# Hybrid trunk on one core: the second delta mixer's tail merged with the second triangular inverse, and sixteen steps of memory pieces in the second layer's first mixer

## The chip, the core and the metric

The kernel runs on one core of a Trainium2 chip. Its engines work side by side and meet at semaphores: TensorE (PE, matrix products), VectorE (DVE), ScalarE (ACT), GpSimd (POOL, unused here) and SyncE (SP), whose queue issues the weight transfers in order. The time is that of the device for one execution, in microseconds (us); before the change three runs gave a median of 1926.84 us (1923.26 to 1929.85).

## The reference, cut to what matters

Two decoder layers over 256 tokens of width 1024. Each layer projects its input once, runs four mixers on groups of 256 columns, projects their outputs, attends to a memory of 256 tokens and ends with a feed-forward part (dense, then experts).

```python
for l in range(DEPTH):
    p = rmsnorm(x, norm_mix[l]) @ w_in[l]
    y_a = hgrn2_mixer(...)          # first mixer: gated linear recurrence, levels of doubling width
    y_b = gated_deltanet_mixer(...) # second: needs (I + lower)^-1 per chunk and head
    y_c = rglru_mixer(...)          # RG-LRU: elementwise scan
    y_d = rwkv7_mixer(...)          # RWKV-7: needs a second inverse of the same kind
    x = x + concatenate([y_a, y_b, y_c, y_d]) @ w_out[l]
    k, v = mem_n @ xattn_wk[l], mem_n @ xattn_wv[l]     # depends on the memory alone
    x = x + cross_attention(rmsnorm(x, norm_xattn[l]), k, v)
    x = x + (swiglu(...) if l % 2 == 0 else moe_swiglu(...))
# delta rule inside y_b, per chunk: u, w = solve((I + lower), [v*b, k*b*exp(g)])
# v_new = u - w @ state ; o = (q*exp(g)) @ state + scores @ v_new ; state = decay*state + k^T @ v_new
```

## The kernel before

Every engine has its own program, written out by hand in one order; there is no scheduler. `ahead(n)` on ACT and DVE splits weight chunks up to number n: a chunk arrives as f32 in one of three buffers `raw`, ACT rounds it into `whi`, DVE puts the rest into `wlo` by a subtraction (128x2048), and PE multiplies with both. SP's queue loads chunks and memory pieces in the order of `plan_chunks`; a load waits until the buffer's user of three loads earlier is done: for a chunk that is `w_lo` (DVE's subtraction), for a memory piece `kv_done` (its last matmul).

**Memory pieces.** Keys and values of the memory are computed in eight pieces per layer, numbered 0 to 7 here, each of eight steps `kv(l, i, ks)`. A step is two matmuls of 128x256; it depends on nothing but the piece's load, and so it is put on PE wherever PE would wait. `kv_put(l, i)` is ACT's copy of a finished piece. Piece 6 is worked off in the RWKV tail. The load order around it is, in layer 0: piece 3, output chunk 0, piece 4, piece 5, output chunk 1, piece 6, chunks 2 and 3; in layer 1: piece 4, output chunk 0, piece 5, output chunk 1, piece 6, chunks 2 and 3. So in layer 0 output chunk 1 takes the buffer of output chunk 0 and piece 6 follows it on the queue; in layer 1 piece 6 itself takes the buffer of output chunk 0.

**The mixers.** `hgrn(l)` is the first mixer with seven levels. Then `inverse(2l)` inverts the delta mixer's 64x64 triangles and `inverse(2l+1)` RWKV's. An inverse has an entry (transposes, a first group) and levels 1 to 6. In a level PE forms the inner products (`inv_t`), DVE masks them (`inv_t1`), PE forms the outer ones (`inv_p`), DVE adds them to X (`inv_xy`) and ACT copies Y (`inv_c`), for two groups g. `after(v)` on PE and DVE's `beside(v)` are other work of the level. Between the inverses stood the delta mixer's tail, a serial chain on PE, DVE and ACT: `solve(6, 0)` -> ACT copies (`gd_us`) -> state -> DVE masks (`state_bd`) -> `gd_km` -> DVE subtracts (`gd_r1`) -> `solve(6, 1)` -> ACT -> `outputs` -> squares -> `head_ss`. RWKV's operands were formed on DVE (`rwkv_operands`), and its first scores (`rk_sc`) and their mask (`inv_n`) started the second inverse. After that inverse comes the RWKV tail, again a chain, with the steps of piece 6 between its parts.

In layer 0, `hgrn` held sixteen steps (pieces 0 and 1, four ahead of the levels), in layer 1 eight. The low part of output chunk 0 was made on DVE in level 1 of the second inverse:

```python
                    if v == 1:
                        ahead(first_chunk["w_out", l] + 1)
```

Of the kernel before, what the change touches and what calls it, by code (L numbers as in the profile page):

```python
# [14 lines left out]
P = 128  # L15
# [3 lines left out]
TT = SEQ // P  # L19
# [90 lines left out]
def build(nc, A, out):  # L110
# [14 lines left out]
    with ExitStack() as ctx:  # L125
# [188 lines left out]


# [92 lines left out]
        KV_BANK = [[7, 6, 7, 7, 7, 7, 2, 1], [3, 1, 7, 7, 7, 7, 2, 3]]  # L408
# [67 lines left out]
        def _(act):  # L476
# [180 lines left out]
            def hgrn(l):
                for v in range(LEVELS):
# [29 lines left out]
                    if v == 6:  # L688
                        kv_put(l, 1 + l)
# [22 lines left out]
            def head_rms(l):  # L712

                act.wait_ge(S("o_full"), 2 * l + 2)
                a(tmp(6), ps[:, 6, :], ACT.Square).then_inc(S("o_sq"), 1)
                act.wait_ge(S("rk_ops"), l + 1)
                act.wait_ge(S("o_ss"), 2 * l + 2)
                a(tmp(7), ps[:, 5, :], ACT.Ln, scale=1.0 / HD, bias=epsc(0))
                a(tmp(7), tmp(7), ACT.Exp, scale=-0.5).then_inc(S("o_rn"), 1)
                inverse_turned(2 * l + 1)  # L720
                inverse_first(2 * l + 1)
                table("natural_log")

# [15 lines left out]
            def deltanet(l):  # L739
                inverse_level(2 * l, 2)  # L740
                kv_put(l, 2 + l)
# [7 lines left out]
                kv_put(l, 3 + l)  # L749
                for t in range(TT):  # L750
                    act.wait_ge(S("gd_u"), 2 * l + t + 1)
                    a(tmp(6)[:, 256 * t:256 * t + 256], ps[:, 6, 256 * t:256 * t + 256], ACT.Copy).then_inc(S("gd_us"), 1)
                head_rms(l)
                inverse_level(2 * l + 1, 1)
                kv_put(l, 4 + l)
                inverse_level(2 * l + 1, 2)
                inverse_level(2 * l + 1, 3)
                inverse_level(2 * l + 1, 4)
                inverse_level(2 * l + 1, 5)
                ahead(first_chunk["w_out", l] + 2)  # L760
# [207 lines left out]
        def _(dve):  # L968
# [305 lines left out]
            def inverse(i, after=None):  # L1274

                N, X, Y, T1 = mt(3), X_INV, mt(5), mt(0)
                for v in range(LEVELS):
                    for g in range(2):
                        s_ = slice(256 * g, 256 * g + 256)
                        if v == 0:  # L1280
                            for u in HALVES:
                                tt(many(T1[u, s_]), many(N[u, 512 * g:512 * g + 512])[:, :, u], rep(level_b(0)[u], 4), ALU.mult)
                            tt(many(Y[:, s_]), rep(ident_b[:, :], 4), many(T1[:, s_]), ALU.subtract).then_inc(S("inv_xy"), 1)
# [38 lines left out]

            def rwkv_operands(l):

                tt(pt(B_K), K_KK, K_EM, ALU.mult).then_inc(S("rk_kb"), 1)
                tt(pt(A_I), pt(D_R), K_E, ALU.mult)
                tt(cm(pt(B_V))[:, :, 0:P], cm(pt(D_K))[:, :, 0:P], cm(pt(A_Q))[:, :, 0:P], ALU.mult)
                tt(cm(pt(B_V))[:, :, P:], cm(pt(D_R))[:, :, P:], cm(pt(A_Q))[:, :, P:], ALU.mult)
                tt(cm(pt(C_X))[:, :, 0:P], cm(K_KA)[:, :, 0:P], cm(pt(A_Q))[:, :, 0:P], ALU.mult)
# [1171 lines left out]
```

## Time and profile before

| | us |
|---|---|
| three runs, median | 1926.84 (1923.26 to 1929.85) |
| the profiled execution | 1923.63 |
| its span, first to last instruction | 1921.8 |
| PE busy | 1844.5 |
| DVE busy | 1436.4 |
| ACT busy | 1153.5 |
| mean granted TensorE clock | 0.988 of full |

The mixers of layer 0 lie at 113.8 to 262 us of the span, those of layer 1 at 652.8 to 795; projections, attention and feed-forward fill the rest, the experts from 915 on. A row of a timeline gives start, duration, engine, line, what is written from what, and in brackets the engine's idle time before it with what ended it. One f32 matmul shows as two records.

### The profile page before, as it was taken

To read this page: it belongs to the slowest core of one execution; us is meant where nothing else is said; L and a number is where in the kernel's file an instruction comes from. 1 tells how busy PE (TensorE), PEld (TensorE's weight loads), DVE (VectorE), ACT (ScalarE), POOL (GpSimd) and SP (SyncE) were. 2 spreads that over 40 slices of the span, in tenths; PEclk is the share of its full clock that TensorE was granted. 3 is DMA by queue.
4 is the path that set the end of the run, shared out by engine and by line. 5 is a ranking of instruction groups with operands and counts; after the bars stand their busy time and mean duration, and the time that the engine had idled before them with its cause. 6 is when DMAs were issued, how large, how long until landed. Compare 5 with 4: busy or idle time off the path is not lost.

```text
span 1921.8 us, 30255 instructions
## 1 busy us (share of the span) xinstructions
PE 1844.5 (96%) x12776; PEld 1589.5 (83%) x12777; DVE 1436.4 (75%) x1475; ACT 1153.5 (60%) x1129; POOL 0.2 (0%) x4
## 2 busy tenths in 40 slices
PE   7999999999999988996999999999999999999996
PEld 6988789999999877895788888888888888888884
DVE  6876654544458876545889989899898998989985
ACT  6565344434344653444677777677776777767774
POOL 0000000000000000000000000000000000000000
PEclk9999999999999999998999999999999999999998
DMA  7512224455555211234799999999999999999992
GB/s 247 162 60 68 68 88 168 164 189 181 176 173 172 66 46 68 88 132 167 288 365 368 361 333 377 350 370 365 326 386 341 365 372 332 382 364 340 371 374 87
DMA packets 239452, 466.02 MB, mean 242 GB/s; under 512 B 11856, under 2 KB 87760, under 8 KB 239312
## 3 DMA queue, kind: packets, MB, share of 16 engines
q1 hardware_dynamic: 239168, 463.93, 67.6%
q8 instruction: 103, 1.69, 0.4%
q14 instruction: 37, 0.30, 0.0%
q10 hardware_dynamic: 144, 0.11, 0.0%
HBM read 462.95 MB, written 1.05 MB: 241 GB/s over the span
## 4 chain that ended last, share of the span: by engine, by line
PE 92%; DVE 6%; issue 1%; ACT 1%; DVEq 0%; DMA 0%; ACTq 0%
PE ps L2265 32%; PE ps L1696 16%; PE ps L2275 16%; PE ps L1681 15%; PE ps L1716 8%; PE ps L2321 2%; PE ps L2296 1%; PE ps L1761 1%; DVE MT L974 1%; PE ps L2336 1%; DVE TMP L974 0%; DVE MT L977 0%; DVE hT_lo L980 0%; DVE MT L1216 0%; PE ps L1786 0%
## 5 line engine op out<-in xcount | busy, mean ns | idle before, releaser
L1458 DVE TENSOR_TENSOR wlo<-raw,whi 128x2048 fp32r<-128x2048 f32 x140 | 320.5, 2291 | 55.8 <-ACT whi L843 55.6
L843 ACT ACTIVATE whi<-raw 128x2048 fp32r<-128x2048 f32 x140 | 268.9, 1922 | 120.8 <-PE ps L2275 71.3
L987 DVE TENSOR_TENSOR wlo<-raw,whi 128x2048 fp32r<-128x2048 f32 x85 | 194.5, 2289 | 83.8 <-ACT whi L494 83.7
L1458 DVE TENSOR_TENSOR wlo<-PT,whi 128x2048 fp32r<-128x2048 f32 x84 | 192.1, 2292 | 31.2 <-ACT whi L843 30.2
L494 ACT ACTIVATE whi<-raw 128x2048 fp32r<-128x2048 f32 x85 | 162.2, 1908 | 80.1 <-PE ps L1716 31.9
L2265 PE MATMUL ps<-whi,hE_hi 128*128 128x512 f32 x672 | 185.4, 398 | 2.4 <-DVE hE_lo L1527 2.4
L843 ACT ACTIVATE whi<-PT 128x2048 fp32r<-128x2048 f32 x84 | 161.4, 1922 | 34.8 <-PE ps L2265 34.2
L2265 PE MATMUL ps<-wlo,hE_hi 128*128 128x512 f32 x672 | 180.1, 390 | 0.0
L2265 PE MATMUL ps<-whi,hE_lo 128*128 128x512 f32 x672 | 179.8, 389 | 0.0
L2265 PEld LDWEIGHTS ps<-wlo,hE_hi 128*128 128x128 f32 x672 | 126.2, 188 | 27.2
L2265 PEld LDWEIGHTS ps<-whi,hE_lo 128*128 128x128 f32 x672 | 126.1, 188 | 26.7
L2265 PEld LDWEIGHTS ps<-whi,hE_hi 128*128 128x128 f32 x672 | 122.0, 188 | 24.8 <-DVE hE_lo L1527 2.6
L2275 PE MATMUL ps<-whi,act_hi 128*128 128x512 f32 x336 | 130.8, 389 | 1.4 <-DVE act_lo L1502 1.4
L2275 PE MATMUL ps<-whi,act_lo 128*128 128x512 f32 x336 | 130.8, 389 | 0.0
L2275 PE MATMUL ps<-wlo,act_hi 128*128 128x512 f32 x336 | 130.7, 389 | 0.0
L1696 PE MATMUL ps<-hT_hi,whi 128*128 128x256 f32 x848 | 120.8, 285 | 0.0
L1696 PE MATMUL ps<-hT_hi,wlo 128*128 128x256 f32 x848 | 119.0, 283 | 0.0
L1696 PE MATMUL ps<-hT_lo,whi 128*128 128x256 f32 x848 | 119.0, 283 | 0.0
L1696 PEld LDWEIGHTS ps<-hT_hi,whi 128*128 128x128 f32 x848 | 110.1, 192 | 2.3 <-issue 1.4
L1696 PEld LDWEIGHTS ps<-hT_lo,whi 128*128 128x128 f32 x848 | 109.4, 192 | 0.0
L1696 PEld LDWEIGHTS ps<-hT_hi,wlo 128*128 128x128 f32 x848 | 109.4, 192 | 0.0
L485 ACT ACTIVATE MT<-ps 128x256 f32<-128x256 f32 (+2 forms) x94 | 43.9, 467 | 104.8 <-PE ps L1696 51.6
(301 smaller groups left out, 3337.8 us busy)
## 6 DMA issues: line engine op xcount, KB each, us to landing
raw<-in_moe_w_up SPq DMA_DIRECT2D x111, 1024.0 KB, 7.1
PT<-in_moe_w_down SPq DMA_DIRECT2D x56, 1024.0 KB, 6.7
PT<-in_moe_w_gate SPq DMA_DIRECT2D x55, 1024.0 KB, 7.0
TMP<-in_moe_w_gate SPq DMA_DIRECT2D x55, 1024.0 KB, 6.9
raw<-in_moe_w_down SPq DMA_DIRECT2D x55, 1024.0 KB, 5.9
raw<-in_w_in SPq DMA_DIRECT2D x28, 1024.0 KB, 5.5
raw<-in_ffn_w_gate SPq DMA_DIRECT2D x11, 1024.0 KB, 5.4
raw<-in_ffn_w_up SPq DMA_DIRECT2D x11, 1024.0 KB, 5.5
```

The costliest lines, as they stand in the source:

```text
L485: return chain.link(lambda: nc.scalar.activation(o, i, f, **kw))
L494: nc.scalar.activation(whi[i % SPL][:, :], raw[d % RAW][:, :], ACT.Copy).then_inc(S("w_hi"), 1)
L843: nc.scalar.activation(ex_hi[m % XSPL], ex_raw[m % XRAW], ACT.Copy).then_inc(S("w_hi"), 1)
L974: return chain.link(lambda: V.tensor_tensor(o, x0, x1, op))
L987: V.tensor_tensor(wlo[i % SPL][:, :], raw[d % RAW][:, :], whi[i % SPL][:, :].bitcast(F32), ALU.subtract).then_inc(S("w_lo"), 1)
L1458: V.tensor_tensor(ex_lo[m % XSPL], ex_raw[m % XRAW], ex_hi[m % XSPL].bitcast(F32), ALU.subtract).then_inc(S("w_lo"), 1)
L1681: return Signalled(pe.matmul(o, lhsT, rhs, start=start, stop=stop, skip_group_check=True))
L1696: ins = pe.matmul(ps[:, bank, SEQ * m:SEQ * m + SEQ], wp[a_][:, k, P * m:P * m + P], src[b_][:, k, :], start=i == 0 and k == 0, stop=last)
L1716: ins = pe.matmul(ps[:, 4 + 2 * t + hf, :], src(b_, kk, t), wp[a_][:, kk, 512 * hf:512 * hf + 512], start=first and kk == 0 and i == 0, st ...
L2265: ins = pe.matmul(ps[:, bank, :], h_[b_][:, X_K * i + k, :], wp[a_][:, k, :], start=i == 0 and n_ == 0 and k == 0, stop=i == 1 and n_ == 2 ...
L2275: ins = pe.matmul(ps[:, 4 + hf, :], act_[b_][:, P * (TM_ROWS * i + kk):P * (TM_ROWS * i + kk) + P], wp[a_][:, kk, 512 * hf:512 * hf + 512] ...
L2321: ins = pe.matmul(g_tokens(c), xs[:, t, P * c:P * c + P], oneh[:, P * t:P * t + P], start=t == 0, stop=t == 1)
```

## The change

1. The delta mixer's tail moves into the levels of the second inverse: PE does `solve(6, 0)` at v 0, the state at v 1, `gd_km` at v 2, `solve(6, 1)` at v 3, `outputs` at v 4, `head_ss` at v 5. DVE's and ACT's parts move with it. Y of the second inverse gets another place (`y_work`), because `mt(5)` still holds the first inverse's result; the delta output is copied out of PSUM (`g_out`).
2. RWKV's first scores are made at the end of the first inverse, in bank 4, and its operands are spread over DVE's `beside`.
3. In layer 1 the pieces are dealt as in layer 0: pieces 2 and 3 in `hgrn` (sixteen steps), piece 4 from there to level 2 of the first inverse, none at its levels 3 to 6, piece 5 in the second inverse. In layer 0 pieces 4 and 5 both lie in the second inverse.
4. The splits of the output chunks move: DVE's low part of chunk 0 stands after the second inverse, chunk 1's after the RG-LRU work, which in turn stands after the RWKV state's mask; ACT's split of chunk 1 stands in the RWKV tail.

The load order of SP is the same. The diff, cut to its core:

```diff
@@ ACT
-                    if v == 3:
-                        rel_part(l, 0)
-                        if l == 0:
-                            kv_put(0, 0)
+                    if v == 3:
+                        rel_part(l, 0)
+                        kv_put(l, 2 * l)
...
             def rwkv(l):
+                i = 2 * l + 1
+                inverse_turned(i)
+                inverse_first(i)
+                gdn_right(l, 0)
+                inverse_level(i, 1)
...
+                inverse_level(i, 3)
+                gdn_right(l, 1)
+                inverse_level(i, 4)
+                act.wait_ge(S("o_full"), 2 * l + 2)
+                a(tmp(6), ps[:, 6, :], ACT.Square)
+                a(g_out(l), ps[:, 6, :], ACT.Copy).then_inc(S("o_sq"), 1)
+                inverse_level(i, 5)
...
+                        act.wait_ge(S("y_put"), 4 * l + 2)
+                        ahead(first_chunk["w_out", l] + 2)
                     act.wait_ge(S("rk_u"), 2 * l + t + 1)
@@ DVE, rwkv
                     if v == 0:
-                        head_out(l, 1, ps[:, 6, :], tmp(7), lambda c: pc("gdn_norm", l), pt(B_Z), 1)
+                        tt(pt(A_I), pt(D_R), K_E, ALU.mult).then_inc(S("rk_kb"), 1)
...
                     if v == 1:
-                        ahead(first_chunk["w_out", l] + 1)
+                        dve.wait_ge(S("state"), 3 * l + 2)
...
                     if v == 2:
                         mask(l, 1, 4, mt(1), strict).then_inc(S("rk_m"), 1)
+                        dve.wait_ge(S("gd_km"), l + 1)
+                        tt(tmp(4)[:, 256:512], tmp(4)[:, 256:512], ps[:, 6, 256:512], ALU.subtract).then_inc(S("gd_r1"), 1)
...
+                mask(l, 0, 4, mt(3), strict).then_inc(S("inv_n"), 1)
                 inverse(2 * l + 1, after=beside)
+                ahead(first_chunk["w_out", l] + 1)
+                head_out(l, 1, g_out(l), tmp(7), lambda c: pc("gdn_norm", l), pt(B_Z), 1)
+                dve.wait_ge(S("state"), 3 * l + 3)
...
                 rglru(l, LEVELS)
                 chain.settle()
                 ahead(first_chunk["w_out", l] + 2)
@@ PE, hgrn and deltanet
-                    if l and 1 <= v < 5:
-                        kv(1, 2, [v + 3])
-                    if l == 0 and v < 2:
-                        kv(0, 0, range(5, 8) if v else [4])
-                    if l == 0 and 2 <= v < 6:
-                        kv(0, 1, [2 * v - 4, 2 * v - 3])
+                    if v < 2:
+                        kv(l, 2 * l, range(5, 8) if v else [4])
+                    if 2 <= v < 6:
+                        kv(l, 2 * l + 1, [2 * v - 4, 2 * v - 3])
...
+                    if v == LEVELS - 1:
+                        pe.wait_ge(S("rk_kb"), 2 * l + 1)
+                        scores(4, pt(B_Q), pt(B_K)).then_inc(S("rk_sc"), 1)
@@ PE, rwkv
+                k4 = ([0, 1, 2], [3, 4], [5, 6, 7], [], [], [], [])
+                k5 = ([], [], [], [0, 1, 2], [3, 4], [5], [6, 7]) if l == 0 else ([0], [1], [2], [3], [4], [5], [6, 7])
```

**The order on DVE, layer 0, second inverse.** Before, level 1 and the beginning of level 2; `wlo` is the low part of output chunk 0.

```order
L974 TENSOR_TENSOR MT<-ps,con16b 128x256 [waits y_put,inv_t]
L974 TENSOR_TENSOR MT<-ps,con16b 128x256 [waits inv_t1,inv_t]
L987 TENSOR_TENSOR wlo<-raw,whi 128x2048 [waits w_hi]
L974 TENSOR_TENSOR MT<-MT,ps 128x256 [waits inv_t1,inv_p]
L974 TENSOR_TENSOR MT<-MT,ps 128x256 [waits inv_xy,inv_p]
L974 TENSOR_TENSOR MT<-ps,con16b 128x256 [waits inv_xy,inv_t]
L974 TENSOR_TENSOR MT<-ps,con16b 128x256 [waits inv_t1,inv_t]
L980 SCALAR_TENSOR_TENSOR MT<-ps,con 128x1024 [waits inv_t1,rk_sc]
```
Now, the end of that inverse (level 6, RWKV's last mask, the two copies that end the inverse) and what follows.

```order
L986 TENSOR_SCALAR MT<-ps 64x256 [waits inv_xy,inv_t]
L986 TENSOR_SCALAR MT<-ps 64x256 [waits inv_t1,inv_t]
L989 SCALAR_TENSOR_TENSOR MT<-ps,con 128x1024 [waits inv_t1,rk_sc]
L1311 COPY MT<-ps 64x256 [waits rk_m,inv_p]
L1311 COPY MT<-ps 64x256 [waits inv_xy,inv_p]
L996 TENSOR_TENSOR wlo<-raw,whi 128x2048 [waits w_hi]
L983 TENSOR_TENSOR TMP<-spare_hi_50,TMP 128x512 [waits inv_xy,o_rn]
L989 SCALAR_TENSOR_TENSOR TMP<-TMP,par,PT 128x256 [waits dve_step] x2
L1210 CAST hT_hi<-TMP 128x512 [waits dve_step]
```
The subtraction of 128x2048 moved from between the products and the adds of level 1 to behind the last copy.

**The order on PE, layer 0, from level 6's second group to piece 6.** `memT,raw` or `raw,memT` of 128x256 are steps; the transposes are `con,PT`. Before:

```order
L1681 MATMUL ps<-MT 64x64 [waits inv_t1,inv_c]
L1681 MATMUL ps<-MT 64x64 x3
L1684 MATMUL ps<-con,PT 128x128 [waits y_put]
L1684 MATMUL ps<-con,PT 128x128 x3
L1681 MATMUL ps<-raw,memT 128x256 [waits raw_in1,rk_m,inv_xy]
L1681 MATMUL ps<-raw,memT 128x256 x3
L1681 MATMUL ps<-TMP,MT 128x64 [waits rk_vk]
L1681 MATMUL ps<-TMP,MT 128x64 x3
```
Now:

```order
L1689 MATMUL ps<-MT 64x64 [waits inv_t1,inv_c]
L1689 MATMUL ps<-MT 64x64 x3
L1689 MATMUL ps<-raw,memT 128x256 [waits raw_in2,raw_in1]
L1689 MATMUL ps<-raw,memT 128x256 x3
L1692 MATMUL ps<-con,PT 128x128 [waits o_rn]
L1692 MATMUL ps<-con,PT 128x128 x3
L1689 MATMUL ps<-raw,memT 128x256 [waits rk_ops,raw_in1,rk_m,inv_xy]
L1689 MATMUL ps<-raw,memT 128x256 x3
L1689 MATMUL ps<-TMP,MT 128x64 [waits rk_vk]
```
Two steps of piece 5 stand between the level and the transposes, and the first steps of piece 6 wait on `rk_ops` too; they wait for their load (`raw_in1`) in both.

**The order on PE, layer 0, the entry of the second inverse.** `PT` of 128x128 are RWKV's first scores, `MT,con` of 64x64 the transposes behind the mask. Before:

```order
L1681 MATMUL ps<-PT 128x128 [waits rk_kb]
L1681 MATMUL ps<-PT 128x128 x7
L1681 MATMUL ps<-TMP,con 128x512 [waits o_sq]
L1681 MATMUL ps<-raw,memT 128x256 [waits raw_in1]
L1681 MATMUL ps<-raw,memT 128x256 x3
L1681 MATMUL ps<-MT,con 64x64 [waits inv_n]
L1681 MATMUL ps<-MT,con 64x64 x15
```
Now, from piece 3's last steps on, at the end of the first inverse:

```order
L1689 MATMUL ps<-memT,raw 128x256 [waits raw_in2,kv_put]
L1689 MATMUL ps<-memT,raw 128x256 x3
L1689 MATMUL ps<-PT 128x128 [waits rk_kb]
L1689 MATMUL ps<-PT 128x128 x7
L1689 MATMUL ps<-MT,con 64x64 [waits inv_n,inv_xy]
L1689 MATMUL ps<-MT,con 64x64 x15
```
Between scores and transposes stood the sums of squares (`TMP,con`) and two steps of piece 4; now they follow each other.

## Rows read from the trace of the kernel before

**Rows 1.** Page, part 1: engine, busy us, share, instructions.
```profile
PE 1844.5 (96%) x12776; PEld 1589.5 (83%) x12777; DVE 1436.4 (75%) x1475; ACT 1153.5 (60%) x1129; POOL 0.2 (0%) x4
```

**Rows 2.** Stretches: length, busy us (instructions) by engine, PE clock, DMA share, GB/s.
```profile
113.80:149.80 36.00, 32.29 (x425) 26.98 (x425) 29.39 (x55) 17.80 (x32) 0.00 (x0) 0.95 0.20 61
...
184.30:235.30 51.00, 46.92 (x812) 38.56 (x810) 28.22 (x52) 15.81 (x28) 0.00 (x0) 1.00 0.25 84
652.80:689.30 36.50, 27.64 (x393) 22.95 (x392) 29.96 (x56) 17.19 (x31) 0.00 (x0) 0.86 0.11 31
...
725.70:767.90 42.20, 37.34 (x772) 31.68 (x771) 27.81 (x51) 15.50 (x27) 0.00 (x0) 1.00 0.21 77
```

**Rows 3.** Timeline of SP's queue (start, us): chunk 1 and piece 6, both layers.
```profile
208.91 0.37 SPq L431 DMA_DIRECT2D raw<-in_w_out  x1
209.32 0.47 SPq L431 DMA_DIRECT2D raw<-in_xattn_wv  x1
...
748.37 0.37 SPq L431 DMA_DIRECT2D raw<-in_xattn_wv  x1
```

**Rows 4.** Transfers at piece 6, layer 0, then layer 1: KB, us from issue to landing.
```profile
raw<-in_xattn_wv SPq DMA_DIRECT2D x1, 1024.0 KB, 7.4
...
raw<-in_xattn_wv SPq DMA_DIRECT2D x1, 1024.0 KB, 5.2
```

**Rows 5.** Timeline of PE, layer 0, delta tail, second inverse, piece 6.
```profile
186.22 1.28 PE L1681 MATMUL ps<-TMP,MT 64*64 64x64 f32 x16
...
195.55 1.16 PE L1681 MATMUL ps<-PT 64*128 64x128 f32 x16
...
197.60 1.89 PE L1681 MATMUL ps<-raw,memT 128*128 128x256 f32 x8
199.42 1.15 PE L1681 MATMUL ps<-MT,con 64*64 64x64 f32 x32
...
205.00 1.48 PE L1681 MATMUL ps<-MT 64*64 64x64 f32 x34
...
209.51 1.13 PE L1681 MATMUL ps<-raw,memT 128*128 128x256 f32 x4 [1.16 <-ACT vA L485]
...
222.68 1.22 PE L1681 MATMUL ps<-MT 64*64 64x64 f32 x64 [0.15 <-DVE MT L974]
...
231.22 2.46 PE L1681 MATMUL ps<-MT 64*64 64x64 f32 x32
233.62 0.66 PE L1684 MATMUL ps<-con,PT 128*128 128x128 f32 x4
235.32 3.63 PE L1681 MATMUL ps<-raw,memT 128*128 128x256 f32 x8 [1.04 <-DVE MT L1301]
```

**Rows 6.** Timeline of PE, layer 1, second inverse: a bare level, and piece 6.
```profile
752.43 2.52 PE L1681 MATMUL ps<-MT 64*64 64x64 f32 x96 [1.07 <-DVE MT L974]
...
767.86 1.14 PE L1681 MATMUL ps<-raw,memT 128*128 128x256 f32 x2 [1.04 <-DVE MT L1301]
```

**Rows 7.** Timeline of ACT, layer 1, first inverse: the copies of level 4.
```profile
716.62 0.86 ACT L485 ACTIVATE MT<-ps 128x256 f32<-128x256 f32 x2
```

**Rows 8.** Timeline of DVE, layer 0, second inverse and what follows.
```profile
206.60 2.28 DVE L987 TENSOR_TENSOR wlo<-raw,whi 128x2048 fp32r<-128x2048 f32 x1
...
231.93 0.96 DVE L977 TENSOR_SCALAR MT<-ps 64x256 f32<-64x256 f32 x2 [3.19 <-PE ps L1681]
233.00 1.23 DVE L980 SCALAR_TENSOR_TENSOR MT<-ps,con 128x1024 f32<-128x1024 f32 x1
234.32 0.94 DVE L1301 COPY MT<-ps 64x256 f32<-64x256 f32 x2
235.37 0.69 DVE L974 TENSOR_TENSOR spare_lo<-spare_lo 128x512 f32<-128x512 f32 x1
```

**Rows 9.** Stretches as in rows 2: at piece 6 of layer 0, and at the router.
```profile
235.50:238.90 3.40, 3.40 (x10) 2.66 (x10) 3.23 (x6) 0.09 (x1) 0.00 (x0) 0.50 0.01 2
901.10:914.80 13.70, 5.47 (x26) 5.32 (x27) 11.99 (x35) 1.49 (x2) 0.00 (x0) 0.50 0.43 140
```

More of the change, by code:

```diff
@@ L313, in build, with y_work, g_out @@
         X_INV, NT, NC = H(1), H(8), H(9)
+        def y_work(i):
+            return g_rel(i // 2)[:, 0:512] if i % 2 else mt(5)[:, 0:512]
+        def g_out(l):
+            return g_rel(l)[:, 512:1024]
         def col(a, n=1):
@@ L1386, in beside @@
+                    if v == 3:
+                        tt(cm(pt(B_V))[:, :, 0:P], cm(pt(D_K))[:, :, 0:P], cm(pt(A_Q))[:, :, 0:P], ALU.mult)
+                        tt(cm(pt(B_V))[:, :, P:], cm(pt(D_R))[:, :, P:], cm(pt(A_Q))[:, :, P:], ALU.mult)
                     if v == 4:
                         mask(l, 2, 4, PT[:, 0:1024], incl).then_inc(S("rk_m"), 1)
+                    if v == 5:
+                        tt(K_B, pt(D_R), pt(D_K), ALU.mult)
+                        for c in range(2):
+                            s_ = slice(256 * c, 256 * c + 256)
+                            ts(K_B[:, s_], K_B[:, s_], pc("rwkv_r_k", l, c), ALU.mult).then_inc(S("rk_ops"), 1 if c else 0)
@@ L1979, in head_ss @@
                 pe.wait_ge(S("o_sq"), 2 * l + which + 1)
-                mm(ps[:, 5 if which else 6, :], bdones, squares).then_inc(S("o_ss"), 1)
+                mm(ps[:, 6, :], bdones, squares).then_inc(S("o_ss"), 1)
             def inverse(i, after=None):
-                N, X, Y, T1 = mt(3), X_INV, mt(5), mt(0)
+                N, X, Y, T1 = mt(3), X_INV, y_work(i), mt(0)
                 SWAPPED = tuple(zip(HALVES, HALVES[::-1]))
@@ L2077, in deltanet @@
-                solve(6, 0, tmp(4)).then_inc(S("gd_u"), 1)
-                pe.wait_ge(S("kv_put"), 2 * NH * l + 4 + l)
-                kv(l, 4 + l, [0])
-                pe.wait_ge(S("gd_us"), 2 * l + 1)
-                for c in range(2):
-                    mm(ps[:, 1, P * c:P * c + P], tmp(3)[:, P * c:P * c + P], tmp(6)[:, P * c:P * c + P]).then_inc(S("state"), 1 if c else 0)
-                kv(l, 4 + l, [1])
-                pe.wait_ge(S("state_bd"), 3 * l + 2)
-                for c in range(2):
-                    mm(ps[:, 1, 256 + P * c:256 + P * c + P], g_kbe(l)[:, 256 * c + P:256 * c + 256], tmp(3)[:, 256 + P * c:256 + P * c + P]).then_inc(S("gd_km"), 1 if c else 0)
@@ L2107, in turn_operands @@
+                    kv(l, 5, k5[v])
+                    if v == 0:
+                        pe.wait_ge(S("rk_rn"), l + 1)
+                        solve(6, 0, tmp(4)).then_inc(S("gd_u"), 1)
                     if v == 1:
-                        pe.wait_ge(S("rk_ops"), l + 1)
-                        pe.wait_ge(S("o_rn"), 2 * (l + 1))
+                        pe.wait_ge(S("gd_us"), 2 * l + 1)
+                        for c in range(2):
+                            mm(ps[:, 6, P * c:P * c + P], tmp(3)[:, P * c:P * c + P], tmp(6)[:, P * c:P * c + P]).then_inc(S("state"), 1 if c else 0)
@@ L2110, in turn_operands @@
                         scores(4, pt(A_G), pt(B_K)).then_inc(S("rk_sc"), 1)
+                    if v == 2:
+                        pe.wait_ge(S("state_bd"), 3 * l + 2)
+                        for c in range(2):
+                            mm(ps[:, 6, 256 + P * c:256 + P * c + P], g_kbe(l)[:, 256 * c + P:256 * c + 256], tmp(3)[:, 256 + P * c:256 + P * c + P]).then_inc(S("gd_km"), 1 if c else 0)
                     if v == 3:
+                        pe.wait_ge(S("gd_r1"), l + 1)
+                        solve(6, 1, tmp(4)).then_inc(S("gd_u"), 1)
```

133 lines of the change are left out of this document (53 added, 80 removed).

## The prediction

> **What bounds the kernel now.** I read the page's busy times and its chain first: TensorE (PE) is busy 96% of the span [rows 1]. So outside the two mixers nothing can move, and inside them only PE's gaps and PE's own work count. The change keeps PE's work (every matmul is only moved) and touches four stretches, which the view by stretch gives [rows 2]: the first mixer of layer 0 (36.0 us, PE busy 32.29) and of layer 1 (36.5 us, PE 27.64), and the stretch from the end of the first inverse to the third mixer's tail, 51.0 us (PE 46.92) in layer 0 and 42.2 us (PE 37.34) in layer 1. Everything that a perfect merge could win is PE's idle time there: 4.1 us and 4.9 us, and up to 8.9 us in layer 1's first mixer. Then I read what starts the weight transfers, since the merge moves a vector operation on which a transfer waits: the DMA issues and their landings [rows 3, 4].
>
> **Part 1, sixteen steps in the first mixer's levels (layer 1).** Eight more steps of memory pieces go there, each two matmuls; eight records (two steps) take 1.89 to 1.93 us [rows 5], so a step is 0.96 us and the eight are 7.7 us. The two layers show what they cost: with all sixteen (layer 0) the stretch is 36.0 us, with eight fewer 36.5 us, while VectorE (DVE) is busy 29.39 and 29.96 us in them [rows 2]. DVE sets the pace there; the steps fill gaps. Cost: -0.5 us.
>
> **Part 2, what these steps leave behind.** Layer 1's first inverse loses the same 7.7 us of steps at its levels 3 to 6. It doesn't get them back in full. A level without filler waits about 1.07 us for DVE's add [rows 6], and ScalarE's exponentials run on as before: its copies of level 4 start only at 716.62 [rows 7], and level 5's second half needs them. With the copies done at 717.5, level 5 ends at about 718.2, DVE (now with one more product, 0.69 us as such a one in [rows 8], ahead of its adds) frees level 6 at 719.8, and level 6 (2.4 us, as in [rows 5]) ends at 722.2. The RWKV scores that move here cost 1.1 us [rows 5], so PE is through at 723.3, where before it began the tail at 725.7: -2.4 us. In layer 0 the steps stay, the extra product pushes PE from 184.3 + 1.93 to 186.4, and the scores end at 187.5.
>
> **Part 3, the merged stretch.** From the end of those scores to the start of level 6 of the second inverse, with durations of [rows 5]:
> - Entry 5.1 us: the mask now follows the scores with nothing under it (1.23 us by [rows 8], with latency 1.35), transposes 1.15, then the next group, 2.0 of work with 0.65 of waiting for DVE's first products. Before, squares and two steps covered the mask.
> - The delta net's tail 5.5 us: from 186.22 to 195.55 are 9.33 us, less four steps (3.84). Three scores 3.3, the head sums 0.96.
> - Levels: level 1 3.35 (205.00 to 208.35, where the idle time before 209.51 begins), levels 2 to 5 each 1.15 + 0.15 + 1.15 = 2.45.
> - Steps: fourteen in layer 0 (13.4), six in layer 1 (5.8).
> - A new wait at level 2: the product that DVE subtracts is the last thing PE does there; a subtraction and an add of about 0.45 each (operations of this size in [rows 8]: 0.47) with their latencies leave PE idle 1.0.
> Sum 42.4 us in layer 0 (187.5 to 229.9) and 34.8 us in layer 1 (723.3 to 758.1, or 757.6 with part 1). Then PE has level 6, two steps and the transposes, 2.4 + 1.9 + 0.66 = 5.0: it is ready for the last piece (piece 6) at 234.9 and 762.6. Before, it was at 235.32 and 767.86. So by PE alone the change is worth -0.4 and -5.3 us.
>
> **Part 4, what the move does to a transfer.** Piece 6 is issued late, and this decides. On SP's queue, in layer 0, it stands behind the second output chunk, which reuses the buffer of the first and waits until DVE has made its low part; in layer 1 piece 6 waits for that low part itself. Before, DVE made it inside level 1 of the second inverse (206.60, 2.28 us [rows 8]), and the issues stand right behind: 208.91 and 209.32 in layer 0, 748.37 in layer 1 [rows 3], some 26 and 19 us before PE wants them. Now this subtraction stands behind the whole inverse. DVE is through with the inverse 4.05 us after level 6 begins (231.22 to 234.32 + 0.94 [rows 5, 8]; the same products, mask and copies): at 233.95 and 761.65. Then 2.3 us of subtraction. Layer 0: chunk issued at 236.3, piece 6 at 236.7, landing 7.4 us later as in [rows 4], at 244.1; PE idles 9.2 us. Layer 1: issue at 764.0, landing 5.2 us later [rows 4], at 769.2; PE idles 6.6 us. PE does nothing else meanwhile, because the step that waits is next in its order. So piece 6 starts 244.1 - 235.3 = +8.8 us in layer 0 and 769.2 - 767.9 = +1.3 us in layer 1; parts 1 to 3 are in these two numbers.
>
> **Part 5, behind the wait.** The gated output, the copies and a table load of ScalarE (ACT) fit under the idle time. DVE's RG-LRU work (from 235.37 on in [rows 8], some 4 us) and the second low part (2.3) now come after the state, still ahead of the head sums that DVE must answer: hidden, at worst 1 us. ACT's split of the second chunk (1.9 us) now stands ahead of the copy for the last state: it ends at 5.9 us from the start of piece 6, the copy at 6.3, wanted at 6.4. Nothing, or 1 us per layer. The granted clock: piece 6's first two steps took 3.63 us at 0.50 before [rows 5, 9], against 1.89 at full rate, a loss of 1.7 us. After an idle time of 9 us they will be at half rate again. I take no difference.
>
> The Trainium skill, TensorE: Matmul & The Clock Gate, section "HAM oscillation — how this bites in real kernels", says that waits for a DMA drop the clock to half and that the matmuls behind them pay. The trace agrees: a stretch with two long gaps was granted 0.50 for 13.7 us [rows 9]. By that rule alone each new wait adds a loss; by the row of piece 6 the loss was there already.
>
> **Sum.** By layer: 0 is -0.4 by PE and +9.2 by the wait, 1 is -5.3 and +6.6: +8.8 + 1.3 = +10.1 us. The profiled execution took 1923.63 us (span 1921.8), 3.2 below the median of the three runs. Its like would then take 1933.7; against the median it is 1926.84 + 10.1 = 1936.9. I forecast 1937.
>
> Bounds. Layer 0's shift can't be under 5.6: if all PE gaps of my walk vanished (1.35 + 0.65 + 1.0 + 0.2), level 6 would begin at 226.7 and everything from DVE's end on follows. Layer 1 by the same gaps between -2 and +3. Upward: each half-rate interval more costs 1.7, two or three are possible; the copy and the sum 1 each. So +3 to +16.
>
> **Rivals.**
> A, the forecast: +5 to +14. For it: the issues stand directly behind the low part in [rows 3, 8]. Chance 0.62, nearly all of it over 0.3%.
> B, more half rate: the entry wait (1.35 + 0.65), unfilled levels in layer 1 and the idle times of 9 and 7 us draw three more intervals, 3 x 1.7 = +5: 1942. For it: [rows 9]. Against: layer 1's second inverse had bare levels [rows 6] without a drop until its end. Chance 0.15.
> C, the clock goes the other way: before, half-rate intervals lie in both mixers (granted 0.95 and 0.86 over the first mixers [rows 2]) and one at piece 6 in each layer. If the two at piece 6 go (2 x 1.7) and the walk's waits shrink by 2 us per layer, +10.1 - 7.4 = +2.7: 1930. Chance 0.17.
> D, faster: the first low part is early enough for piece 6. Then no new wait, and parts 1 to 3 stand alone: -0.4 - 5.3 = -5.7, 1921. It decides at the moment of issue: piece 6 must be issued 5.2 to 7.8 us before PE is ready, at 227.1 in layer 0 and 757.4 in layer 1; DVE would have to be through with the chunk before level 6, against its order. Chance 0.06.
> The change doing nothing at all is ruled out by the new order of DVE.
>
> **Chances.** 0.3% (5.8 us), about what a measurement of this kernel can tell from no change, puts the bounds at 1921.1 and 1932.6. Slower: A 0.60 and B 0.15, 0.75. Same: 0.02 of A and C, 0.19. Faster: D, 0.06. The range takes A, B and most of C: 1928 to 1944.
>
> **What would show it.** The issue of piece 6 at the end of DVE's subtraction, and an idle time of 6 to 10 us on PE ahead of the first matmuls of piece 6, released by a DMA, in both layers, longer in layer 0. Layer 1's first mixer near 36.0 us with PE busy above 34. Idle time of 1.3 us ahead of the second inverse's transposes and of 1 us at its level 3. If the stretch 184.3 to piece 6 in layer 0 isn't longer than 56 us, part 4 is wrong; if the first mixer of layer 1 grows, part 1 is.

## The result, and the profile after

| | before | after |
|---|---|---|
| runs measured together, median (us) | 1924.65 (5 runs, 1923.26 to 1929.85) | 1941.22 (5 runs, 1939.49 to 1946.26) |
| the profiled execution, its span | 1923.63, 1921.8 | 1946.26, 1944.5 |
| mean granted TensorE clock | 0.988 | 0.979 |

The change makes the kernel slower: ratio 1.0084, 95% interval 1.0066 to 1.0102, or +16.6 us by the medians. The forecast was 1937 with a range of 1928 to 1944. The profiled execution of after is the slowest of its five, 5 us above their median; two more profiles of the same kernel stand below.

The page of after: PE works 9 us longer than in [rows 1] with the same 12776 instructions, so some of them ran slower; the chain is PE for 90%, and a DMA has a share in it.

```profile
PE 1853.7 (95%) x12776; PEld 1599.7 (82%) x12777; DVE 1436.2 (74%) x1475; ACT 1153.9 (59%) x1131; POOL 0.2 (0%) x4
...
PE 90%; DVE 6%; ACT 1%; issue 1%; DMA 1%; DVEq 0%; SPq 0%; ACTq 0%
```

PE of after in layer 0, from RWKV's scores to piece 6, as [rows 5]:

```profile
186.31 1.16 PE L1689 MATMUL ps<-PT 64*128 64x128 f32 x16
188.89 1.15 PE L1689 MATMUL ps<-MT,con 64*64 64x64 f32 x32 [1.42 <-DVE MT L989]
...
213.03 1.21 PE L1689 MATMUL ps<-MT 64*64 64x64 f32 x32 [1.04 <-DVE MT L983]
...
232.77 2.47 PE L1689 MATMUL ps<-MT 64*64 64x64 f32 x32
235.17 1.99 PE L1689 MATMUL ps<-raw,memT 128*128 128x256 f32 x8
237.00 0.60 PE L1692 MATMUL ps<-con,PT 128*128 128x128 f32 x4
247.18 3.75 PE L1689 MATMUL ps<-raw,memT 128*128 128x256 f32 x8 [9.58 <-DMA raw<-in_xattn_wv]
```

The waits at the entry (1.42) and at level 3 (1.04) are there, and PE stands 9.58 us ahead of piece 6. Layer 1, from the last levels of the first inverse on, as [rows 6]:

```profile
725.66 3.74 PE L1689 MATMUL ps<-MT 64*64 64x64 f32 x128 [1.26 <-DVE MT L983]
730.70 1.16 PE L1689 MATMUL ps<-MT 64*64 64x64 f32 x48 [1.30 <-ACT MT L491]
732.93 3.33 PE L1689 MATMUL ps<-MT 64*64 64x64 f32 x32 [1.07 <-DVE MT L983]
736.20 2.08 PE L1689 MATMUL ps<-PT 64*128 64x128 f32 x16
739.69 1.61 PE L1689 MATMUL ps<-MT,con 64*64 64x64 f32 x25 [1.42 <-DVE MT L989]
...
779.06 0.60 PE L1692 MATMUL ps<-con,PT 128*128 128x128 f32 x4
786.34 3.75 PE L1689 MATMUL ps<-raw,memT 128*128 128x256 f32 x8 [6.68 <-DMA raw<-in_xattn_wv]
```

Two things stand here: the second wait, 6.68 us, and scores that take 2.08 us in place of 1.16, because they run at half rate. DVE of after in layer 0, as [rows 8]:

```profile
235.88 0.94 DVE L1311 COPY MT<-ps 64x256 f32<-64x256 f32 x2
236.74 2.27 DVE L996 TENSOR_TENSOR wlo<-raw,whi 128x2048 fp32r<-128x2048 f32 x1
```

And SP's queue in both layers, as [rows 3]. The issue follows the end of `wlo` (239.01) as closely as before, but 30 us later, and in layer 1 20 us later once its own shift of 12.6 us is taken off:

```profile
239.04 0.37 SPq L437 DMA_DIRECT2D raw<-in_w_out  x1
239.45 0.47 SPq L437 DMA_DIRECT2D raw<-in_xattn_wv  x1
...
781.10 0.37 SPq L437 DMA_DIRECT2D raw<-in_xattn_wv  x1
```

Stretches of after (columns as in [rows 2], the clock third from the end), all granted 0.50: the entry of layer 0's second inverse, the wait for piece 6 with what follows it, and in layer 1 the end of the first inverse with the next entry, and again piece 6.

```profile
190.80:197.60 6.80, 6.80 (x47) 5.81 (x44) 2.19 (x5) 1.19 (x2) 0.00 (x0) 0.50 0.02 6
242.00:252.20 10.20, 5.02 (x16) 4.33 (x17) 0.00 (x0) 0.00 (x0) 0.00 (x0) 0.50 0.71 261
733.50:743.70 10.20, 8.78 (x108) 8.36 (x107) 6.76 (x14) 3.58 (x6) 0.00 (x0) 0.50 0.01 2
784.70:791.50 6.80, 5.16 (x17) 4.44 (x18) 0.00 (x0) 0.00 (x0) 0.00 (x0) 0.50 0.50 192
```

With 3.4 us each in the two first mixers that is 40.8 us at half rate inside the mixers, against 20.4 us in the profile of before. To place the loss I use the first matmul of the first output chunk in each layer, with which the output projection starts. In before it starts here, and layer 1's mixers begin with the transposes at 652.84:

```profile
253.40 0.58 PE L1716 MATMUL ps<-whi,hT_hi 128*128 128x512 f32 x1
...
652.84 0.60 PE L1684 MATMUL ps<-con,PT 128*128 128x128 f32 x4
...
785.95 0.58 PE L1716 MATMUL ps<-whi,hT_hi 128*128 128x512 f32 x1
```

In after the two are at 266.00 and 805.23, so +12.6 us by the end of layer 0's mixers and +19.3 by the end of layer 1's. The rest of this profile's 22.6 us lies at the router, where 24 us were granted 0.50 in place of 13.7 us in [rows 9].

### The profile page after: what moved, and what is told of

It is laid out like the page before. It is cut to its first block, busy times and chain, and to the rows that moved or that the text cites. A ratio compares the mean times of both kernels' runs of the same rounds, so it can differ in the third digit from the quotient of the medians.

```text
span 1944.5 us, 30260 instructions
## 1 busy us (share of the span) xinstructions
PE 1853.7 (95%) x12776; PEld 1599.7 (82%) x12777; DVE 1436.2 (74%) x1475; ACT 1153.9 (59%) x1131; POOL 0.2 (0%) x4
## 4 chain that ended last, share of the span: by engine, by line
PE 90%; DVE 6%; ACT 1%; issue 1%; DMA 1%; DVEq 0%; SPq 0%; ACTq 0%
PE ps L2273 31%; PE ps L1704 16%; PE ps L2283 16%; PE ps L1689 15%; PE ps L1724 8%; PE ps L2329 2%; PE ps L2304 1%; PE ps L1769 1%; DVE MT L983 1%; PE ps L2344 1%; DMA raw<-in_xattn_wv 1%; DVE wlo L996 0%; DVE TMP L983 0%; DVE hT_lo L989 0%; DVE MT L1225 0%
## 5 line engine op out<-in xcount | busy, mean ns | idle before, releaser
L491 ACT ACTIVATE MT<-ps 128x512 f32<-128x512 f32 (+2 forms) x78 | 37.7, 483 | 84.0 <-PE ps L1704 51.2
```

What stands on the lines that cost most here:

```text
L491: return chain.link(lambda: nc.scalar.activation(o, i, f, **kw))
```

## The experiments

Medians in us; a shift is the start of the first output chunk against before's, layer 0 and layer 1, in the profiled execution.

| run | median (runs) | ratio to before, 95% | shifts |
|---|---|---|---|
| after | 1941.22 (5) | 1.0084 (1.0066 to 1.0102) | +12.6, +19.3 |
| e1_low_part_early | 1918.09 (7) | 0.9963 (0.995 to 0.9977) | -3.3, -4.4 |
| e2_before_low_part_late | 1940.63 (4) | 1.009 (1.0069 to 1.0111) | +8.4, +18.3 |
| e3_entry_covered | 1935.85 (5) | 1.006 (1.0046 to 1.0073) | +8.1, +12.1 |
| e4_early_and_covered | 1915.34 (6) | 0.9949 (0.9931 to 0.9968) | -5.1, -11.3 |
| e5_early_and_old_deal | 1921.87 (12) | 0.9988 (0.9976 to 1.0) | -3.0, -3.4 |
| e6_low_part_level5 | 1924.21 (10) | 1.0006 (0.9993 to 1.002) | +2.6, +0.7 |
| e8_early_covered_km | 1913.26 (6) | 0.9945 (0.9928 to 0.9962) | -5.6, -13.9 |
| e9_wait_filled | 1947.04 (5) | 1.0113 (1.0094 to 1.0133) | +13.1, +22.9 |
| e10_wait_filled_short | 1935.82 (5) | 1.005 (1.0037 to 1.0064) | +7.4, +7.5 |
| e11_after_again | 1942.84 (1) | - | +8.9, +16.2 |
| e12_after_third | 1939.26 (1) | - | +8.7, +15.5 |

These runs fall into batches, each with its own runs of before; their medians are 1924.65 (for after), 1925.64 (e1, e2, e3, e5), 1924.46 (e4, e6, e8, e9) and 1926.54 (e10), and e11 and e12 stand beside a single run of 1921.63. The batches differ by up to 2.1 us, so kernels of different batches are compared by their distance from before: after +16.6, e1 -7.6, e2 +15.0, e3 +10.2, e4 -9.1, e5 -3.8, e6 -0.3, e8 -11.2, e9 +22.6, e10 +9.3.

**Where the low part stands.** In after, DVE's low part goes back to a level of the second inverse, everything else stays:

```diff
@@ DVE, beside, v == 3
+                        chain.settle()
+                        ahead(first_chunk["w_out", l] + 1)
@@ behind the inverse
-                ahead(first_chunk["w_out", l] + 1)
```

> The changed kernel with one edit: DVE's low part of output chunk 0 is made at level 3 of the second inverse, not behind it. Theory T (the two waits for piece 6 and the half-rate intervals make the loss): PE's waits of 9.6 us (layer 0) and 6.7 us (layer 1) at piece 6 vanish, and with them some of the half-rate time behind them (up to 2 x 1.7); time 1941.2 - 16.3 - 0 to 3.4 = 1921 to 1925, about the kernel before. Rival M (the merge itself is slower, and the transfer only stands where another wait would): another wait appears at piece 6 and the time stays above 1932.

Measured 1918.09, 0.4% under before, 3 us under what I expected; from +16.6 to -7.6 us it is 24.1 us. PE no longer waits for piece 6: its steps (third row) follow the transposes directly. They take 1.89 us for eight records, in both layers, where before took 3.63 [rows 5]: the half rate that before had at piece 6 is gone too. SP issues it at 214.81 and 748.36.

```profile
231.58 1.99 PE L1690 MATMUL ps<-raw,memT 128*128 128x256 f32 x8
233.41 0.60 PE L1693 MATMUL ps<-con,PT 128*128 128x128 f32 x4
233.85 1.89 PE L1690 MATMUL ps<-raw,memT 128*128 128x256 f32 x8
```

The other half of the proof puts the late low part into the kernel before:

```diff
@@ before, DVE, beside
-                    if v == 1:
-                        ahead(first_chunk["w_out", l] + 1)
@@ behind the inverse
                 inverse(2 * l + 1, after=beside)
+                ahead(first_chunk["w_out", l] + 1)
                 rglru(l, LEVELS)
```

> The kernel before with the same one edit the other way: the low part of output chunk 0 behind the second inverse, all else as before. T: piece 6 of layer 0 is issued at about 238.0 and lands 7.4 us later, a wait of 10 us; in layer 1 issued at 770.1, landing 5.2 us later, 7.5 us; 1924.65 + 17.6 = 1942, as slow as the changed kernel. M: the order of the low part alone does nothing, 1925.

Measured 1940.63, +15.0 us and so nearly as slow as after, with the same kind of wait in both layers, 1.7 and 1.9 us longer than in after:

```profile
244.05 3.38 PE L1680 MATMUL ps<-raw,memT 128*128 128x256 f32 x8 [11.29 <-DMA raw<-in_xattn_wv]
...
786.14 3.69 PE L1680 MATMUL ps<-raw,memT 128*128 128x256 f32 x8 [8.62 <-DMA raw<-in_xattn_wv]
```

So the place of one vector subtraction turns a gain of 0.4% into a loss of 0.8%. The third place tried is level 5:

```diff
@@ DVE, beside, v == 5
+                        chain.settle()
+                        ahead(first_chunk["w_out", l] + 1)
@@ behind the inverse
-                ahead(first_chunk["w_out", l] + 1)
```

> The changed kernel with DVE's low part of output chunk 0 made at level 5 of the second inverse, between e1 (level 3) and the changed kernel (behind level 6). It tests the moment from which the wait decides: piece 6 must be issued 7.7 us (layer 0, behind chunk 1) or 5.2 us (layer 1) before PE is ready. T: DVE gets to it some 8 us before PE is ready in either layer, is through 2.3 us later, and its adds of level 5 come 2.3 us later, where PE has steps, scores and head sums to do. So a short wait of 1 to 3 us in layer 0 and 0 to 1 in layer 1: e1 + 1 to 4 = 1919 to 1922. Rival (any place inside the inverse does): 1918 without a wait on the transfer.

Measured 1924.21, 2 us above what I expected, and by the distances from before 7.3 us above e1, where I expected 1 to 4. DVE in layer 0:

```profile
227.66 2.29 DVE L996 TENSOR_TENSOR wlo<-raw,whi 128x2048 fp32r<-128x2048 f32 x1
229.98 0.95 DVE L983 TENSOR_TENSOR MT<-MT,ps 64x256 f32<-64x256 f32 x2
```

PE, level 6 and piece 6:

```profile
230.46 2.46 PE L1690 MATMUL ps<-MT 64*64 64x64 f32 x32 [0.29 <-DVE MT L983]
...
237.98 2.59 PE L1690 MATMUL ps<-raw,memT 128*128 128x256 f32 x8 [2.69 <-DMA raw<-in_xattn_wv]
```

The subtraction now runs ahead of the add that frees level 6, which now waits 0.29 us (it starts 1.3 us later than in e1, 229.18, but 0.9 us of that stand in this profile from its first mixer on), and piece 6, issued at 230.39, still comes 2.7 us late in layer 0. In layer 1 (issued at 764.98) it is in time. Late is not a matter of yes or no: each layer has its own limit.

**The entry of the second inverse.** Two steps go between the scores and the transposes, and in layer 1 piece 4 is thinned out over more levels for it. The core:

```diff
@@ PE, beside the first inverse
-                        kv(l, 2 * l + 2, [2, 3])
+                        kv(l, 2 * l + 2, [2] if l else [2, 3])
...
-                        kv(l, 2 * l + 2, [4, 5])
+                        kv(l, 2 * l + 2, [3] if l else [4, 5])
...
-                    if l == 0 and v >= 3:
+                    if l and v == 3:
+                        kv(l, 4, [5])
+                    if l == 0 and 3 <= v < LEVELS - 1:
...
                         scores(4, pt(B_Q), pt(B_K)).then_inc(S("rk_sc"), 1)
+                        kv(l, 4 if l else 3, [6, 7])
```

> The changed kernel, with RWKV's first scores ahead of the last two steps of the first inverse's filler, so that these cover the mask, and in layer 1 the steps of piece 4 spread over levels 0 to 3 with two kept for that place. T: the idle time of 1.4 us ahead of the second inverse's transposes goes in both layers, and if it is what draws the half-rate interval there (6.8 us in layer 0, 10.2 us in layer 1, worth up to 3.4 and 5.1 us), that goes too: 1941.2 - 2.8 - 3 to 8 = 1931 to 1936, with both waits at piece 6 as long as before. Rival K (the half-rate interval comes from the sparse last levels, whatever the entry does): only the gaps go, 1938 to 1940, with half-rate intervals still at about 191 and 734 us.

Measured 1935.85, +10.2 us, which is 6.4 less than after. PE in layer 0 has no gap left where after has 1.42 us; in layer 1 the level before the scores ran at half rate again:

```profile
183.97 1.16 PE L1689 MATMUL ps<-PT 64*128 64x128 f32 x16
185.06 1.99 PE L1689 MATMUL ps<-memT,raw 128*128 128x256 f32 x8
186.99 1.15 PE L1689 MATMUL ps<-MT,con 64*64 64x64 f32 x32
...
726.24 3.66 PE L1689 MATMUL ps<-MT 64*64 64x64 f32 x32 [2.00 <-DVE MT L983]
```

The time is in the range of theory T, but its sign is there in layer 0 alone. Even there the covering isn't shown to have brought the clock back: e11 and e12 below have full rate at layer 0's entry with nothing covered.

Both edits together:

> e1 and e3 together: low part at level 3, and the last two steps of the first inverse's filler behind RWKV's first scores, layer 1's piece 4 spread over levels 0 to 3. T: the gains add: 1918.1 - (1941.2 - 1935.9) = 1912.8, within 2. Rival: e3's gain was clock behind the waits for piece 6, which e1 has taken already; then e4 is at 1916 to 1918.

Measured 1915.34, between the two expectations. By the distances from before, covering is worth 1.6 us on e1 and 6.4 us on after. The two idle times of 1.42 us make 2.8; what lies under or over that I put to the clock and to the scatter between batches, and the runs don't settle it.

**The deal of the memory pieces.** e1 with layer 1's old deal (eight steps in the first mixer, pieces 3 and 4 in the first inverse), PE's part of it:

```diff
@@ PE, hgrn
-                    if v < 2:
-                        kv(l, 2 * l, range(5, 8) if v else [4])
-                    if 2 <= v < 6:
-                        kv(l, 2 * l + 1, [2 * v - 4, 2 * v - 3])
+                    if l and 1 <= v < 5:
+                        kv(1, 2, [v + 3])
+                    if l == 0 and v < 2:
+                        kv(0, 0, range(5, 8) if v else [4])
+                    if l == 0 and 2 <= v < 6:
+                        kv(0, 1, [2 * v - 4, 2 * v - 3])
@@ PE, beside the first inverse
-                    if l == 0 and v >= 3:
-                        pe.wait_ge(S("kv_put"), 3)
-                        kv(0, 3, range(2 * v - 6, 2 * v - 4))
+                    if v >= 3:
+                        pe.wait_ge(S("kv_put"), 2 * NH * l + 3 + l)
+                        kv(l, 3 + l, range(2 * v - 6, 2 * v - 4))
```

> As e1_low_part_early, but layer 1's memory pieces dealt as in the kernel before: eight steps in its first mixer's levels instead of sixteen, piece 4 at levels 3 to 6 of the first inverse. T: against e1 the first mixer of layer 1 is no longer than 36.5 us with PE less busy, and the first inverse gets its 7.7 us of steps back and loses its bare levels: +2.9 us without the clock; but the half-rate interval at the entry of layer 1's second inverse (10.2 us) may go or shrink, worth up to 5 us. So between e1 + 3 and e1 - 2. Rival: the sixteen steps stretch the first mixer, and e5 is faster than e1 by more than 3 us.

Measured 1921.87, 0.8 us beyond my range: the new deal is worth 3.8 us, clock included. In e5's profile the half-rate stretch at layer 1's second inverse is gone, although the entry's idle time of 1.42 us is still there; but its first mixer has 13.6 us at half rate, where e1's has 3.4, and takes 38.3 us, where e1's takes 35.9. The merge without the new deal and with the early low part is then 0.1% faster than before, at the edge of what is measured.

**The wait at level 3.** e4, with `gd_km` formed ahead of level 2's steps, so that these cover DVE's answer (cut to its core):

```diff
@@ PE, rwkv
-                    kv(l, 5, k5[v])
+                    if v != 2:
+                        kv(l, 5, k5[v])
...
+                        kv(0, 4, k4[v]) if l == 0 else kv(l, 5, k5[v])
```

> e4 with one more edit in the same sense: at level 2 of the second inverse PE makes the delta mixer's product (gd_km) ahead of that level's steps, so that these cover DVE's subtraction and add. T: the idle time of 1.04 us ahead of level 3 goes in both layers, 2 us: e4 - 2. Rival: the product then waits for DVE (state_bd) ahead of the steps, and nothing is won.

Measured 1913.26, 2.1 us under e4: the two idle times of 1.04 us are gone. This version is the fastest, 0.55% under before.

**The clock behind the waits.** Matmuls that nobody reads fill the wait for piece 6 (36 and 25 of them in e9):

```diff
@@ after, PE, ahead of piece 6
                 pe.wait_ge(S("rk_ops"), l + 1)
+                for n_ in range(25 if l else 36):
+                    mm(ps[:, 1, 0:SEQ], memT[:, n_ % KT, 0:P], memT[:, n_ % KT, :])
                 kv(l, 6, [0, 1])
```

> The changed kernel, with PE kept busy during the waits for piece 6: 36 (layer 0) and 25 (layer 1) matmuls of the memory with itself, 0.24 us each, into a PSUM bank that is free there; nobody reads the products. The transfers come as late as before. It measures the clock's part by itself. T: the half-rate intervals at the waits (242 to 252 and 785 to 792 us) vanish, those of the entries (191, 734) stay; PE then runs piece 6's first steps in 1.9 us instead of 3.75 in each layer and the next parts at full rate: 1941.2 - 2 x 1.7 to 3.4 = 1934 to 1938. Rival (the half rate behind a wait is no cost, since the chain there is bound by ACT and DVE): 1941.

Measured 1947.04, outside what I expected, by a mistake in size: a filler takes 0.43 us, not 0.24, and the fillers ended 5.8 and 4.1 us after piece 6 had landed. Its steps of piece 6 took 1.89 us, though. With fewer of them:

```diff
-                for n_ in range(25 if l else 36):
+                for n_ in range(14 if l else 20):
```

> The kernel after with 20 (layer 0) and 14 (layer 1) matmuls that nobody reads, ahead of the first steps of piece 6, so that TensorE (PE) works through most of the time in which it waits for the transfer. In the run before, 36 and 25 of them took 14.62 and 10.96 us, 0.41 to 0.44 us each, and outlasted the waits by some 5 and 4 us; here they should take about 8.5 and 6.3 us and end ahead of the landings, so that piece 6 starts when it does in the kernel after, with a wait of under 2 us left. Theory T (each wait also costs by the half rate behind it, granted 0.50 over piece 6's first steps): these steps take 1.9 us in place of 3.75, no half-rate stretch stands behind either wait, and the time is 3 to 4 us under the kernel after: 1937 to 1938.5. Rival U (the clock behind the waits costs nothing in the end): the time stays at 1941, +-1.

Measured 1935.82, +9.3 us, which is 7.3 less than after; I expected 3 to 4. PE in both layers:

```profile
234.79 8.80 PE L1689 MATMUL ps<-memT 128*128 128x256 f32 x40
244.44 1.99 PE L1689 MATMUL ps<-raw,memT 128*128 128x256 f32 x8 [0.86 <-DMA raw<-in_xattn_wv]
...
770.23 6.21 PE L1689 MATMUL ps<-memT 128*128 128x256 f32 x28
777.07 1.99 PE L1689 MATMUL ps<-raw,memT 128*128 128x256 f32 x8 [0.63 <-DMA raw<-in_xattn_wv]
```

Stretches of the same kernel: to piece 6 and behind it in layer 0, the entry of the second inverse in layer 1.

```profile
186.30:244.40 58.10, 53.78 (x844) 45.28 (x842) 27.10 (x50) 14.77 (x28) 0.00 (x0) 1.00 0.18 62
244.40:260.80 16.40, 16.36 (x131) 13.70 (x132) 6.61 (x8) 4.42 (x7) 0.00 (x0) 1.00 0.14 54
728.80:742.00 13.20, 11.37 (x254) 9.97 (x253) 6.63 (x14) 3.90 (x8) 0.00 (x0) 1.00 0.02 4
```

Piece 6 starts as late as ever, since the transfer decides that; but its first steps take 1.99 us in place of 3.75, which is 1.8 us in each layer, and this I call shown: nothing else was changed. (From there to the first output chunk it is 16.4 us in both layers, and 17.9 to 18.9 us in the three profiles of after.) The rest of the 7.3 us is another thing. The entries of this execution were at full rate too (first and third stretch), though the program ahead of layer 0's fillers is that of after. So I profiled after twice more.

> The kernel after, unchanged, profiled once more. The first profiled execution of it took 1946.26 us, 5 more than its median, and was granted 0.50 for 40.8 us inside the mixers. Theory T (the half-rate stretches behind the two waits for piece 6 belong to the kernel, those at the entries of the second inverse come and go between executions of the same program): piece 6's first steps take 3.75 us again in both layers, the stretches behind the entries (190.8 and 733.5) are there in one layer or in none, and this execution takes 1938 to 1942 us. Rival U (every half-rate stretch of the first profile belongs to the kernel): the same stretches at the same places, and the five us come from the experts' part alone.

> The same kernel a third time, for the same question. T: 3.75 us for piece 6's first steps in both layers, the stretches at the entries in one layer or in none; U: the same stretches as in the first profile.

Measured 1942.84, 0.8 us above what I expected, and 1939.26. PE of e12 at piece 6:

```profile
243.62 3.75 PE L1689 MATMUL ps<-raw,memT 128*128 128x256 f32 x8 [9.53 <-DMA raw<-in_xattn_wv]
...
782.89 3.75 PE L1689 MATMUL ps<-raw,memT 128*128 128x256 f32 x8 [6.87 <-DMA raw<-in_xattn_wv]
```

Its stretches around layer 1's entry, and over layer 0's second inverse:

```profile
729.60:743.20 13.60, 12.18 (x128) 10.67 (x128) 5.97 (x12) 2.95 (x6) 0.00 (x0) 0.51 0.00 1
...
186.30:234.00 47.70, 44.20 (x796) 37.16 (x793) 22.91 (x45) 11.77 (x25) 0.00 (x0) 1.00 0.07 24
```

Half rate behind both waits is there each time (3.48 to 3.75 us for the eight records). The stretch at layer 0's entry was in the first profile alone; the same idle time of 1.42 us stands there in eight profiles (three of after, e1, e5, e6, e9, e10), and the other seven have no stretch. The one at layer 1's entry does not come and go like that, as theory T had it: it is in all three profiles of after (10.2, 17.1 and 13.6 us) and in those of e1 and e9 (17.1 us each) and e6 (10.2 us); of the kernels with bare levels (levels without steps of a piece) and a bare entry there only e10's profile lacks it. It begins in level 6 of the first inverse, before the scores and the entry's idle time, behind levels 3 to 6 whose steps were moved away. With these levels filled and the entry bare (e5) it is not there. So it goes with the bare levels rather than with the entry, as far as one profile of e5 can say.

## Why the prediction was right, and where it was off

The forecast's direction, its place and the mechanism of its wait (rival A) held; its size did not. Measured +16.6 us is above A's +5 to +14 and above the bound of +16, and 1941.22 is nearest to rival B's 1942, to which I gave 0.15. That the time still lies well inside 1928 to 1944 is in part luck: I added to a median of three runs, 1926.84, and the five runs give 1924.65. On that base the forecast would have been 1934.8, some 6.5 us too low.

The table puts the prediction's steps beside three profiles. Times of layer 1 are less the shift with which its mixers began (12.60 in after, 8.70 in e12, 7.69 in e10, by the transposes that start at 652.84 in before).

| step | forecast | after | e12 | e10 (waits filled, no half rate here) |
|---|---|---|---|---|
| piece 6 issued, layer 0 | 236.7 | 239.5 | 235.9 | 236.8 |
| piece 6 starts, layer 0 | 244.1 | 247.2 | 243.6 | 244.4 |
| first mixer of layer 1, length | 36.0 | 37.5 | 35.9 | 35.9 |
| layer 1's scores end | 723.3 | 725.7 | 723.7 | 722.4 |
| piece 6 issued, layer 1 | 764.0 | 768.5 | 768.8 | 764.2 |
| piece 6 starts, layer 1 | 769.2 | 773.7 | 774.2 | 769.4 |

**Part 1** held in time: from its transposes to those of the delta mixer, layer 1's first mixer takes 35.9 us, before 36.4; the 37.5 of after has a half-rate stretch at its end. My sign for it did not: PE was to be busy above 34 us and was busy 32.18 (e12) and 32.29 (after), as layer 0 had shown all along. I had added 7.7 us of steps to layer 1's 27.64, of which a part was stretched by a clock of 0.86. **Part 2** held: by e10 PE is through with the scores 3.3 us earlier than before (-2.4 forecast), and e5 gives 3.8 us for both parts, forecast 2.9, though with half rate at different places on the two sides. But the bare levels had a price that I didn't put in, see below.

**Part 3** held: the entry's idle time is 1.42 us (1.35 forecast), that of level 3 is 1.04 (1.0). e8 took the second away for what it cost, 2.1 us in the two layers; e3 took the first away and gained 6.4, more than the 2.8 it is long. From the end of the scores until PE is ready for piece 6, layer 0 takes 47.3 us in e12 and e10 (47.4 forecast).

**Part 4** held: issue directly at the end of the subtraction, landing 7.6 and 5.1 us later, waits of 9.58 and 6.68 us against 9.2 and 6.6. e1 and e2 show both ways that this one move decides the sign. Rival D, 1921 for an early low part, is e1's kernel: 1918. It comes that near because two things that D left out offset each other: piece 6's steps at full rate in both layers (1.7 us each), and half rate at the bare levels.

**Part 5** is the step that failed, in its last sentence on the clock, "I take no difference": the sum has no term for half rate at the bare levels, and there it cost 4.5 to 5 us. Of the two places where the clock fell, one is missing from the sum:
- The bare levels in layer 1. In e12, with 13.6 us there at 0.51, piece 6 starts at 774.2, forecast 769.2, 5 us later; in after 4.5. In e10, the same program up to that point but for layer 0's fillers and without the stretch, it starts at 769.4. The prediction had this in rival B, with 0.15, and argued against it by the bare levels of layer 1's second inverse, which ran at full rate [rows 6]. That did not carry over: here idle times of 1.26, 1.30, 1.07 and 1.42 us follow each other. But they do in e10 too, at full rate; what makes the difference between the two places, and between e10 and the others, was not isolated. e1 carries the same loss: in layer 1 its piece 6 starts 0.5 us later than in before, counted from the start of the mixers, where the walk gave 5.3 earlier.
- The half rate behind the waits, by contrast, was sized rightly. Before, one stretch of 3.4 us stood at each piece 6; after a wait it is 6.8 to 10.2 us, part of it inside the wait, where it costs nothing. The loss is the 1.8 us per layer that e10 gives back; as before lost about the same [rows 5], this term was rightly near zero in the sum.

The working then reads: +10.1 by the walk, +5 for the bare levels, which makes 15; measured +16.6 between the medians (+15.5 to +19.3 in the mixers by profile). The kernel whose waits are filled is the cleanest test of the walk: in e10's profile piece 6 starts 9.1 us later than in before in layer 0 and 1.5 us in layer 1, 10.6 in sum. Its first output chunk in layer 1 is only 7.5 us late, because the steps of piece 6 ran at full rate, which the walk doesn't assume. That its median is +9.3 is no test: by the profile 3.2 us more were lost at the router. What stays open is the last 1.5 us and the draw itself: why layer 0's entry was at half rate once and not again.

The Trainium skill, TensorE: Matmul & The Clock Gate, section "HAM oscillation — how this bites in real kernels", says that the matmuls behind a DMA wait pay. Here those behind both waits do: 3.75 us in place of 1.99. The same page of the Trainium skill, section "A second HAM failure mode: psum-queue depth-cycling", tells of a kernel that cycles through PSUM banks and whose frequent short idle times between groups of matmuls bring the clock down as well. Layer 1's bare levels look like that; whether the banks matter here was not tested. I had them in rival B, with too small a chance.

## What to carry to other kernels

When a vector operation moves, list who is queued behind it on the DMA queue, not only who reads its result: one subtraction of 2.3 us, placed behind the inverse instead of in it, held back a transfer in each layer and cost more (15 us, e2) than the rest of the change won (8 us, e1, part of it by the clock at piece 6). Ask of each place that loses its filler what the clock will do there, and price bare levels of small matmuls with some half-rate time rather than nothing. One execution can carry a half-rate stretch that the next one of the same kernel lacks, so a difference that rests on one such stretch is not yet explained.

## What the runs showed of the hardware

- Half rate can come without any long wait. Where bare levels of 64x64 matmuls with idle times of 1.1 to 1.4 us follow each other, six of seven profiles have a stretch of 10.2 to 17.1 us at 0.50; at a wait of 9.6 us it was 10.2. It isn't the idle times alone: e10's profile has the same ones (1.26, 1.27, 1.07 and 1.42 us) at full rate. In e8, with idle times of up to 1.9 us but the entry covered, 3.4 us at half rate were left there.
- At half rate small matmuls slow down nearly as much as large ones: RWKV's scores of 64x128 took 2.08 us against 1.16, piece 6's steps 3.75 against 1.99.
- Work that nobody reads holds the clock at full rate through a wait (1.00 from 186.3 to 260.8 in e10), and is worth it if it ends before the landing; what runs past the landing is lost (5.8 and 4.1 us in e9, which is 6 us slower than after).
